# A hybrid retention and attention block on one core: weight blocks loaded in two transfers of 2 MB in place of four of 1 MB

## The reference, cut to what matters

```python
def reference(x, norm_mix_g, w_in, ret_norm_g, attn_sinks, w_ret_branch, w_attn_branch,
              w_gate, w_out, norm_ffn_g, w_up, w_down, norm_final_g):
    ...
        h = rms_norm(x, norm_mix_g[l])
        proj = jnp.einsum('bsd,de->bse', h, w_in[l])
        rq, rk, rv, rg, aq, ak, av = jnp.split(proj, offsets, axis=-1)
        ...
        ret = (jax.nn.silu(rg.astype(jnp.float32)) * ret).astype(x.dtype)
        y_ret = jnp.einsum('bse,ed->bsd', ret, w_ret_branch[l])
        ...
        y_att = jnp.einsum('bse,ed->bsd', att, w_attn_branch[l])
        gates = jax.nn.sigmoid(jnp.einsum('bsd,de->bse', h, w_gate[l]).astype(jnp.float32))
        ...
        x = x + jnp.einsum('bsd,de->bse', merged, w_out[l])
        h2 = rms_norm(x, norm_ffn_g[l])
        u = jnp.square(jax.nn.relu(jnp.einsum('bsd,df->bsf', h2, w_up[l])))
        x = x + jnp.einsum('bsf,fd->bsd', u, w_down[l])
    return rms_norm(x, norm_final_g)
```

## Time and profile before

| | |
|---|---|
| median of 3 runs | 1492.98 us (1492.97 to 1493.11) |
| the profiled execution | 1492.93 us, its span 1491.1 us |
| PE busy | 1480.5 us, 99% of the span |
| DVE busy | 1084.5 us, 73% |
| ACT busy | 759.3 us, 51% |
| DMA engines, mean busy share | 60% for SP's queue |
| moved through SP's queue | 297.51 MB, most of it weights |

### The profile page before, as it was taken

How to read it: one execution, slowest core, us unless ns; L and a number is a source line. 1 busy time by engine, 2 the same in 40 slices (tenths; PEclk the granted TensorE clock), 3 DMA queues, 4 the chain that set the end, 5 groups by cost and what they waited for, 6 DMA issues and landing times.

```text
span 1491.1 us, 18849 instructions
## 1 busy us (share of the span) xinstructions
PE 1480.5 (99%) x7042; PEld 1292.5 (87%) x7042; DVE 1084.5 (73%) x1396; ACT 759.3 (51%) x1017; POOL 14.3 (1%) x21
## 2 busy tenths in 40 slices
PE   9999999999999999999999999999999999999997
PEld 8888888888888888888888888888888888888886
DVE  7887886554567887777799988558865687549855
ACT  6655655444445555444445555445544555445543
POOL 0000000000000000000000000000000000000000
PEclk9999999999999999999999999999999999999999
DMA  9555455666656665565765666565566566565562
GB/s 326 188 170 198 141 192 174 203 206 239 211 171 196 197 193 199 190 207 197 249 229 186 205 203 225 198 205 182 204 226 198 185 202 230 198 198 184 203 230 88
DMA packets 149687, 299.31 MB, mean 201 GB/s; under 512 B 5120, under 2 KB 5248, under 8 KB 149376
## 3 DMA queue, kind: packets, MB, share of 16 engines
q1 hardware_dynamic: 149056, 297.51, 60.0%
q10 hardware_dynamic: 576, 1.06, 0.2%
HBM read 296.45 MB, written 2.10 MB: 200 GB/s over the span
## 4 chain that ended last, share of the span: by engine, by line
PE 94%; DVE 3%; issue 1%; DMA 1%; SPq 1%; ACT 1%; POOL 0%; POOLq 0%; DVEq 0%
PE acc L429 91%; DVE wlo L1027 1%; DMA raw<-in_w_in 1%; PE pts L477 1%; PE tps L446 1%; PE pts L457 0%; DVE qT L1036 0%; DVE kT L1036 0%; SPq L332 0%; DVE ta_lo L1472 0%; DVE xsq L1229 0%; PE acc L467 0%; PE pts L569 0%; SPq L342 0%; PE tps L585 0%
## 5 line engine op out<-in xcount | busy, mean ns | idle before, releaser
L1027 DVE TENSOR_TENSOR wlo<-raw,whi 128x1024 fp32r<-128x1024 f32 x540 | 654.6, 1224 | 337.9 <-ACT whi L685 334.9
L685 ACT ACTIVATE whi<-raw 128x1024 fp32r<-128x1024 f32 x540 | 566.9, 1056 | 591.6 <-PE acc L429 588.5
L429 PE MATMUL acc<-whi,ta_hi 128*128 128x512 f32 x1308 | 498.5, 381 | 0.6 <-DVE wlo L1027 0.5
L429 PE MATMUL acc<-whi,ta_lo 128*128 128x512 f32 x1308 | 496.2, 379 | 0.0
L429 PE MATMUL acc<-wlo,ta_hi 128*128 128x512 f32 x1308 | 496.1, 379 | 0.0
L429 PEld LDWEIGHTS acc<-whi,ta_hi 128*128 128x128 f32 x1308 | 247.6, 189 | 37.0 <-DVE wlo L1027 1.2
L429 PE MATMUL acc<-whi,tb_hi 128*128 128x512 f32 x736 | 279.3, 379 | 0.0
L429 PE MATMUL acc<-whi,tb_lo 128*128 128x512 f32 x736 | 279.2, 379 | 0.0
L429 PE MATMUL acc<-wlo,tb_hi 128*128 128x512 f32 x736 | 279.2, 379 | 0.0
L429 PEld LDWEIGHTS acc<-whi,ta_lo 128*128 128x128 f32 x1308 | 247.6, 189 | 34.8
L429 PEld LDWEIGHTS acc<-wlo,ta_hi 128*128 128x128 f32 x1308 | 247.7, 189 | 33.9
(11 more groups left out here) (160 smaller groups left out, 666.9 us busy)
## 6 DMA issues: line engine op xcount, KB each, us to landing
raw<-in_w_in SPq DMA_DIRECT2D x64, 1024.0 KB, 5.2
raw<-in_w_up SPq DMA_DIRECT2D x64, 1024.0 KB, 5.4
raw<-in_w_down SPq DMA_DIRECT2D x64, 1024.0 KB, 5.0
raw<-in_w_gate SPq DMA_DIRECT2D x32, 1024.0 KB, 5.4
raw<-in_w_att SPq DMA_DIRECT2D x16, 1024.0 KB, 5.1
raw<-in_w_ret SPq DMA_DIRECT2D x16, 1024.0 KB, 5.0
raw<-in_w_out SPq DMA_DIRECT2D x16, 1024.0 KB, 5.2
raw<-in_w_in SPq DMA_DIRECT2D x7, 512.0 KB, 8.7
```

Of the source, the lines that this page charges most:

```text
L429: last = nc.tensor.matmul(paired(acc[B.parity][:, t, :]), a[:, k, tok], halves_in_turn(b), start=(k == 0 and n == 0), stop=(k == KCH - 1 a ...
L685: nc.scalar.activation(whi[:, s:s + UCH, :], raw[:, u * UCH:(u + 1) * UCH, :], ACT.Copy).then_inc(hi_ready, 1)
L1027: V_.tensor_tensor(wlo[:, s:s + UCH, :], raw[:, u * UCH:(u + 1) * UCH, :], whi[:, s:s + UCH, :].bitcast(f32), ALU.subtract).then_inc(lo_re ...
```

## The change

`load` now moves eight chunks, half a block, 2 MB, and `load_block` calls it twice, h = 0 and h = 1. Of each half the semaphore of its last quarter is kept: `half_full(u)` is `raw_full[1]` for units 0 to 3 and `raw_full[3]` for units 4 to 7. SP waits until the low parts of all four units of that half of the block before are made: `4 * h + 2` in place of `2 * s`. The exception for the first transfer of block 1 now waits for both: the low part of units 0 and 1 (`half_lo`) and that of units 2 and 3. ACT's waits are now on `half_full(u)`; the condition under which it waits is as it was. The pieces of block 0 are loaded as before.

```diff
+        def half_full(u):
+
+            return raw_full[u // 4 * 2 + 1]
+
...
-            def load(B, src, s):
+            def load(B, src, h):
 
                 src = src.rearrange("(k p) n -> p k n", p=P)
                 sp.lower_ap_dma(src)
-                if B.second and s == 0:
+                if B.second and h == 0:
                     sp.wait_ge(half_lo, UCH)
-                elif not B.very_first:
-                    sp.wait_ge(lo_ready, B.number * UNITS + (2 * s - UNITS))
-                sp.dma_start(raw[:, GCH * s:GCH * (s + 1), :],
-                             src).then_inc(raw_full[s], 16)
+                sp.wait_ge(lo_ready, B.number * UNITS + (4 * h + 2 - UNITS))
+                sp.dma_start(raw[:, KCH // 2 * h:KCH // 2 * (h + 1), :],
+                             src).then_inc(half_full(4 * h), 16)
 
             def load_block(B, w, col, row=0):
-                for s in range(LOADS):
-                    load(B, w[ds(row + s * 512, 512), ds(col, COLS)], s)
+                for h in range(2):
+                    load(B, w[ds(row + h * 1024, 1024), ds(col, COLS)], h)
...
                     if B.very_first and u % 2 == 0:
                         act.wait_ge(even_full[u // 2 - 1], 16)
                     elif u % 2 == 0 or B.very_first:
-                        act.wait_ge(raw_full[u // 2], B.number * 16 + 16)
+                        act.wait_ge(half_full(u), B.number * 16 + 16)
...
                     if u % 2 == 0:
-                        act.wait_ge(raw_full[u // 2], B.number * 16 + 16)
+                        act.wait_ge(half_full(u), B.number * 16 + 16)
```

## The result

The changed kernel takes **1496.01 us** (median of 12 runs, 1495.42 to 1497.64) against 1493.03 (12 runs, 1492.81 to 1493.41): 3.0 us or 0.21% slower, ratio 1.0021 with a 95% interval of 1.0014 to 1.0029. The 1496.4 of the prediction lies between, but two of its terms are off, in opposite directions, as will be seen.

What follows compares the result with a forecast made beforehand. PE's matmuls bound the kernel, busy 1480.5 of 1491.1 us. Terms 0 + 3.4 (unit 5's wait and block 1's first half together) + 0 + 0 gave 1496.4 us, 0.23% slower, range 1495.0 to 1499.5.

Steps and rivals of the forecast that it cites:

- the wait at unit 5: Block 0: ACT now waits there for the piece of unit 7, landing at 20.2; PE stalls 2.8 us.
- the two causes: Unit 5's wait in block 0 and block 1's late first half: the 2.8 stall lies inside the 3.4 shift.
- 2 MB take 8.0: Every merged load, issue to landing: 5.1 us for a lone 1 MB plus 2.8 for the rest, taken as 8.0.
- which second halves are late: Later blocks: 25 second halves whose gap between issue and use is under 8.0 us, at cost 0.
- block 28: Shortest gap, 6.2 us: ACT late by 1.8 at unit 4, with 5.4 us of cover, cost 0.
- block 39: Gap of 7.3 us: ACT late by 0.7, with 3.5 us of cover before DVE feels it, cost 0.
- part 4: All later halves: 25 arrive late for ACT, but cover before PE makes the cost 0.
- Part 2: Block 1's first half lands at 27.0 instead of being taken at 23.57, moving L530 by 3.4 us.
- The estimate by bytes alone: Block 1's first half in at 25.7 at 381 GB/s, a shift of 2.1; as the early-landing rival, chance 0.20, 1495.1.
- The Trainium skill's rate: Second case for block 1's first half: in at 25.0, leaving only the 2.2 us from unit 5's wait.
- The clock: Rival at PE's stall in block 0: clock falls to half, 1497.7 for one unit, 1500.3 for two; chance 0.06.

Runs made afterwards that it cites:

- E1: The changed kernel, but unit 5 of block 0 waits for its own piece again, all halves still 2 MB: 1495.89 us against 1493.14.
- E2: The kernel before with one edit, unit 5 of block 0 waiting for the piece of unit 7, transfers still 1 MB: 1496.99 us, ratio 1.0026.
- E3: The changed kernel with unit 5 waiting for its own piece and block 1's first half in two 1 MB transfers as before: 1493.04 us against 1493.14.
- E7: The changed kernel run again, unedited, on the same chip as the next: 1496.98 us, ratio 1.0026 to the kernel before.
- E8: The changed kernel with six small matmuls on zeros ahead of unit 5 of block 0, in PE's stall: 1495.52 us, ratio 1.0017.

## Why the prediction was right, and where it wasn't

**Right, and shown:** the wait at unit 5 (ACT stands 4.25 us there, PE's stall is 3.0 against 2.8), which the list of ACT's waits in the new order tells and the diff easily hides; that the two causes lie over each other and don't add (E1, E2 and the change are all 2.8 to 4 above, not their sum); that 2 MB take 8.0, as a median; which second halves are late, and that they cost 0 (E3), with block 28 late by 1.9 for 1.8 and block 39 by 0.6 for 0.7.

**Off without harm in part 4.** The prediction let every half take 8.0, and the worst is block 34's with 9.5, 3.1 late; block 33's first half was not on the list; and ACT's waits for loads are 58.9 us, not about 40. These waits are longer than the lateness, since they take in what ACT would have waited for PE (4.69 for block 34, of which 1.59 was there before).

**Part 2 was mis-sized.** "I let it land where s = 1 did, at 27.0": it lands at 26.1 when block 0 is on time (E1, 26.14), and L530 moves by 2.56, not 3.4. The 12.9 of the earlier trace rows was one draw, and a late one: in E3 the same transfer s = 1 took 12.1, and the half of 2 MB took 12.0 to 12.2 in the profiles of E1, E7 and E8. The estimate by bytes alone, 25.7, was nearer. The Trainium skill's rate would have had 25.0 (SBUF — State Buffer, "The DMA setup-cost knee"), an estimate that E1's row does not bear out: it is 1.1 later.

**The clock was given too small a chance.** It had 0.06, with a price of 1.3 for one unit at half the clock. The price was about right: 1.7 us of work were lost, and 1.4 of it arrived at the small matmul (E7 against E8). It fell in three of the four profiles with a stall of 2.2 to 3.0 us and nothing in it, and the medians of E7 and E8 differ by 1.5. The argument against it was that the stall of 2.8 is shorter than the 3.0 after which it fell at the end of the program; one such distance is no limit, since in E7 the clock fell after a stall of 2.31. The Trainium skill (TensorE: Matmul & The Clock Gate, "Part 1: The HAM clock gate") speaks of a fall for an idle PE, and these falls, after stalls of 2.31, 2.87 and 3.00, agree with it in kind.

So 1496.4 was near in part by luck: 0.85 too much from the landing, and some 0.5 to 1.5 too little for the clock, cancelled each other. The +2.5 that is left without the clock is what E8 measures (1495.52 - 1492.97 = 2.55), the chain of the squares' sums again. What stays open is how often the clock falls in any set of runs (medians of +3.0 and +4.0 for the same kernel), and E1's single run at 1497.22.

No version beats both kernels: E3 equals the one before, and PE's idle time after the start is as it was.

## What to carry to other kernels

When transfers are merged, look first at the stretch where the queue is full and the consumer already waits: there the consumer of the first half pays for the second (2.6 us here), while an issue 1.7 us later cost nothing. When semaphores are merged too, list every wait with the semaphore that it names, the odd branch included. A load may be issued late as long as it doesn't wait for anything of the load just before it; one step past that, transfer and use stopped overlapping here, and no cover read half by half told the price.

## What the runs showed of the hardware

A stall of TensorE of only 2.2 to 3.0 us, between stretches at full load, was in three profiles of four followed by 3.4 us at a granted clock of 0.5, and the fall came 0.8 to 1.2 us after PE had begun to work again. With matmuls of 1.5 us in the stall, on zeros, the clock stayed at 1.00 in the profile and the median was 1.5 us lower. And the landing of one and the same transfer in the full queue (s = 1, issued at about 14.1) came 12.9 us after its issue in one execution and 12.1 in another. Elsewhere a transfer of 2 MB took 8.0 us as a median and up to 9.6, and 11.7 when three loads of x were on the way.
